# First weight unit of a decoder trunk split in halves on two engines, with the opening of TensorE reordered

## Chip, cores and metric

One core of a Trainium2 chip runs the whole program in one launch. The metric is device time in microseconds (us) of one execution, the median of several. Engines: TensorE (PE), VectorE (DVE), ScalarE (ACT), GpSimd (POOL) and SyncE (SP), which issues the transfers.

## What is computed

Two layers over 512 tokens of width 1024, all in float32. The opening, which the change touches, is the norm of the input and the first columns of the projection `w_in`:

```python
def rms_norm(x, g):
    xf = x.astype(jnp.float32)
    y = xf * lax.rsqrt(jnp.mean(xf * xf, axis=-1, keepdims=True) + NORM_EPS)
    return (y * g.astype(jnp.float32)).astype(x.dtype)

for l in range(DEPTH):                       # DEPTH = 2
    h = h + token_mixer(rms_norm(h, ln1_g[l]), w_in[l], ...)   # starts with u @ w_in
    h = h + hier_moe(rms_norm(h, ln2_g[l]), ...)
return rms_norm(h, final_g)
```

`token_mixer` holds four attention-like branches with gates, `hier_moe` a router and 32 experts.

## The kernel before

A float32 product is made of three fast matmuls (`mm3`, L568 to L570): each operand is split in a high part, rounded to the fast type, and a low part, the rest. High times high, high times low and low times high are summed in PSUM. So each weight unit and each tile of u needs a high part (a ScalarE copy) and a low part (a subtraction) ahead of its matmuls.

`w_in` is cut in units of 256 columns (1024 rows as 8 groups k of 128), which SyncE loads in a ring of four slots `raw`. `split_h(u)` on ScalarE writes `ringH`, `split_l(u)` on GpSimd writes `ringL` (in the same memory as `raw`). Unit 0 ("gv") is used by rows: its halves q = 0 and 1 work on token tiles 0, 1 and then 2, 3, 24 matmuls (8 k x 3) for each tile. Unit 1 ("ga", the low-rank columns) and all later units need all four tiles.

A token tile t (128 tokens) passes through these steps: square sums on ScalarE (`row_squares`), mean on VectorE (`mean_square`), the power -1/2 on GpSimd (`norm_scale`), scaling with the gain `g1` on VectorE (`first_rows`), 8 turns on PE (`norm_transposes`), high part on ScalarE (`norm_h`), low part on VectorE (`norm_low`).

Each engine's program is written out by hand as a sequence with semaphore waits, and an engine handles its instructions strictly in that order. In layer 0 ScalarE's order is: squares 0 and 1, `split_h(0)`, squares 2 and 3, `norm_h` 0 and 1, `split_h(1)`, `norm_h` 2 and 3, then the loop over halves, which begins with `split_h(2)`. GpSimd does scales 0 and 1, `split_l(0)`, scales 2 and 3, `split_l(1)`. PE turns tiles 0 and 1, then waits for the low parts of unit 0 and of tile 0, works on tile 0, turns tile 2 between tiles 0 and 1, and turns tile 3 ahead of tile 2. Layer 1 has orders of its own, since its opening is mixed with the end of layer 0: there half of unit 0 was already subtracted by VectorE (`next_unit_low`, signals `front_high` and `front_low`).

SyncE issues x tile 0, the small constants `cst`, unit 0, `g1`, x tiles 1 to 3, unit 1, ten small constants, units 2 and 3, and a copy of x to DRAM. It doesn't wait for any engine up to there but for x.

In the expert stage `keep_warm` (L934 before) issues matmuls of a constant whose result nobody reads.

## Time and profile before

| | us |
|---|---|
| median of 3 runs | 1482.52 (1477.93 to 1482.81) |
| profiled execution | 1481.1 |
| its span | 1479.3 |
| PE busy | 1395.6 (94%) |
| ACT busy | 473.6 (32%) |
| DVE busy | 430.4 (29%) |
| POOL busy | 489.8 (33%) |

All durations below come from the profiled execution; its clock starts at the span's start. A PE matmul's own duration holds its latency, so matmuls overlap: how fast they run is read from start to start.

### The profile page before, as it was taken

How to read it: one execution, taken by the hardware profiler on the slowest of the kernel's cores; microseconds unless marked ns; L12 is line 12 of the kernel's file. 1: busy time of each engine (PE TensorE's matmuls, PEld its weight loads, DVE VectorE, ACT ScalarE, POOL GpSimd, SP SyncE). 2: the span in 40 equal slices, each digit the busy share in tenths (PEclk: the TensorE clock that was granted, in tenths of full speed). 3: DMA queues.
4: the chain of work that ended last, by engine and by line, in shares of the span. 5: the costliest groups of instructions: out<-in, count | busy, mean ns of one | idle time of the engine just before them, and what ended most of it. 6: DMA issues, size and time to landing. Idle time of an engine off the chain costs nothing.

```text
span 1479.3 us, 18875 instructions
## 1 busy us (share of the span) xinstructions
PE 1395.6 (94%) x7502; PEld 969.5 (66%) x7502; DVE 430.4 (29%) x1042; ACT 473.6 (32%) x818; POOL 489.8 (33%) x241
## 2 busy tenths in 40 slices
PE   5999999999999898988999999999999989998986
PEld 5889877788888633333388888777888874333332
DVE  2232554410122312111333435443102141121114
ACT  4522466632332111111253326765223311111112
POOL 3633433456660111111144343335567301111111
PEclk9999999999999799999999999999999998999999
DMA  7522222224375899999963213222334669999996
GB/s 249 190 86 86 72 72 72 72 89 146 107 267 200 342 414 420 419 420 416 391 241 102 86 58 107 72 72 72 96 139 162 235 232 400 414 420 420 419 414 263
DMA packets 129154, 331.23 MB, mean 224 GB/s; under 512 B 16613, under 2 KB 90421, under 8 KB 105512
## 3 DMA queue, kind: packets, MB, share of 16 engines
q1 hardware_dynamic: 120424, 314.29, 55.7%
q0 software_dynamic: 8640, 15.69, 2.8%
q8 instruction: 62, 1.02, 0.3%
q14 instruction: 28, 0.23, 0.0%
HBM read 312.17 MB, written 33.55 MB: 234 GB/s over the span
## 4 chain that ended last, share of the span: by engine, by line
PE 77%; DMA 16%; DVE 2%; SPq 1%; ACT 1%; issue 1%; POOL 1%; POOLq 0%; DVEq 0%; ACTq 0%
PE ps L568 18%; PE ps L569 17%; PE ps L570 17%; PE ps L956 13%; DMA w<-in_w 12%; DMA yb<-y_dram 2%; PE ps L770 1%; PE ps L750 1%; PE ps L758 1%; PE ps L706 1%; PE ps L948 1%; SPq L467 1%; PE ps L867 1%; DMA x_dram<-hs 1%; DMA hs<-in_x 1%
## 5 line engine op out<-in xcount | busy, mean ns | idle before, releaser
L568 PE MATMUL ps<-uH,ringH 128*128 128x512 f32 x704 | 276.1, 392 | 0.0
L569 PE MATMUL ps<-uL,ringH 128*128 128x512 f32 x704 | 274.6, 390 | 0.0
L570 PE MATMUL ps<-uH,ringL 128*128 128x512 f32 x704 | 274.5, 390 | 0.0
L956 PE MATMUL ps<-w,xT 128*64 128x512 f32 x1024 | 229.0, 599 | 14.7 <-DMA w<-in_w 12.1
L956 PEld LDWEIGHTS ps<-w,xT 128*64 128x64 f32 x1024 | 77.1, 138 | 161.0 <-issue 152.8
L1370 POOL TENSOR_TENSOR ringL<-raw,ringH 128x2048 fp32r<-128x2048 f32 x29 | 133.3, 4606 | 81.8 <-ACT ringH L1098 81.8
L956 PE MATMUL ps<-w,hT 128*64 128x512 f32 x512 | 129.1, 650 | 30.2 <-DMA w<-in_w 18.9
L568 PEld LDWEIGHTS ps<-uH,ringH 128*128 128x128 f32 x704 | 132.6, 188 | 28.6 <-issue 0.7
L570 PEld LDWEIGHTS ps<-uH,ringL 128*128 128x128 f32 x704 | 132.4, 188 | 27.9
L569 PEld LDWEIGHTS ps<-uL,ringH 128*128 128x128 f32 x704 | 132.5, 188 | 27.1
L1416 POOL TENSOR_TENSOR ringL<-raw,ringH 128x2048 fp32r<-128x2048 f32 x32 | 147.1, 4597 | 5.4 <-ACT ringH L1239 5.4
L1447 POOL DMA_INDIRECT y_dram<-yy,toks x28 | 28.2, 1009 | 348.7 <-DVE yy L1904 327.6
L1313 ACT ACTIVATE silu<-ps,slot_w 128x256 f32<-128x256 f32 x32 | 15.1, 473 | 323.8 <-PE ps L956 323.8
L1419 POOL TENSOR_TENSOR merged<-merged,term 128x512 f32<-128x512 f32 x48 | 67.1, 1397 | 149.3 <-DVE term L1721 149.3
L956 PEld LDWEIGHTS ps<-w,hT 128*64 128x64 f32 x512 | 38.6, 148 | 98.3 <-issue 81.6
L1243 ACT ACTIVATE sig<-ps 128x512 f32<-128x512 f32 x64 | 38.3, 598 | 201.1 <-PE ps L570 201.0
L568 PE MATMUL ps<-ringH,uH 128*128 128x256 f32 x320 | 93.4, 292 | 3.5 <-POOL ringL L1370 2.5
L569 PE MATMUL ps<-ringL,uH 128*128 128x256 f32 x320 | 91.0, 284 | 0.0
L570 PE MATMUL ps<-ringH,uL 128*128 128x256 f32 x320 | 91.0, 284 | 0.0
L1721 DVE TENSOR_TENSOR term<-sig,ps 128x512 f32<-128x512 f32 x48 | 32.9, 686 | 198.3 <-PE ps L570 124.4
L1904 DVE SCALAR_TENSOR_TENSOR yy<-xg,first_choice,ps 128x512 f32<-128x512 f32 x56 | 39.3, 744 | 139.7 <-PE ps L956 139.7
L1860 DVE SCALAR_TENSOR_TENSOR hid<-silu,slot_w,ps 128x256 f32<-128x256 f32 x32 | 15.4, 480 | 211.1 <-ACT silu L1313 211.1
(266 smaller groups left out, 2076.5 us busy)
## 6 DMA issues: line engine op xcount, KB each, us to landing
w<-in_w SPq DMA_DIRECT2D x176, 1024.0 KB, 17.4
raw<-in_w_in SPq DMA_DIRECT2D x54, 1024.0 KB, 5.0
w<-in_w SPq DMA_DIRECT2D x32, 512.0 KB, 17.8
raw<-in_w_out SPq DMA_DIRECT2D x8, 1024.0 KB, 5.2
yb<-y_dram SPq DMA_DIRECT2D x8, 1024.0 KB, 15.7
braw<-in_w_branch SPq DMA_DIRECT2D x24, 256.0 KB, 4.4
h_dram<-hs SPq DMA_DIRECT2D x2, 2048.0 KB, 11.8
y_dram<-attT SPq DMA_DIRECT2D x8, 512.0 KB, 9.0
```

The lines of the kernel that those rows point to most:

```text
L568: mm(o, h, rh, start=first, stop=False)
L569: mm(o, h, rl_, start=False, stop=False)
L570: return mm(o, l, rh, start=False, stop=last)
L956: ins = mm(o[r], lhs[:, r], rhs[x], start=first, stop=last, skip_group_check=True)
L1243: fn(sig[:, j % 2, :], bank(b), ACT.Sigmoid).then_inc(bank_freed[b].h, 1)
L1370: gp_.tensor_tensor(ringL[:, s, :], raw[:, s, :], ringH[:, s, :].bitcast(f32), ALU.subtract).then_inc(unit_low.h, 1)
L1416: gp_.tensor_tensor(ringL[:, s, :], raw[:, s, :], ringH[:, s, :].bitcast(f32), ALU.subtract).then_inc(unit_low.h, 1)
L1419: gp_.tensor_tensor(merged[:, j, :], merged[:, j, :], term[:, j % 2, :], ALU.add).then_inc(term_added.h, 1)
L1447: gp_.indirect_dma_start(y_dram, bass.IndirectOffsetOnAxis(toks[:, 1, p:p + 1], axis=0), yy[:], None, bounds_check=2 * S - 1, oob_is_err=F ...
L1721: v.tensor_tensor(term[:, j % 2, :], sig[:, j % 2, :], bank(A[5]), ALU.mult).then_inc(term_ready.h, 1)
L1860: return v.scalar_tensor_tensor(hid[:], silu[:], slot_w[:, 0, col], bank(0)[:, FH:2 * FH], ALU.mult, ALU.mult)
L1904: last = v.scalar_tensor_tensor(yy[:, cc], xg[p % 3][:, cc], first_choice[:, p:p + 1], bank(A[c]), ALU.mult, ALU.add)
```

## The change

- SyncE issues `g1` ahead of unit 0.
- ScalarE, layer 0: unit 0 is split in two halves of 1024 columns (k 0 to 3, k 4 to 7). Order: squares 0, first half, `norm_h(0)`, squares 1, second half, squares 2 and 3, `norm_h(1)`, `split_h(1)`, `norm_h(2)`, `split_h(2)`, `norm_h(3)`. `split_h(2)` was behind `norm_h(3)`.
- VectorE subtracts both halves of unit 0 (`unit_low_half`); GpSimd's `split_l(0)` is gone.
- PE, layer 0: five keep-warm matmuls at the start and five behind the turns of tile 0. The turns of tiles 1 and 2 stand between k 3 and k 4 of tiles 0 and 1. PE waits for the first half of unit 0 ahead of tile 0 and for the second ahead of its k 4.
- `front_high` and `front_low` count one more, since layer 0 now uses them too. Layer 1's orders stay.

```diff
--- before.py
+++ after.py
@@ -269,7 +269,7 @@
     bank_filled = signal("bank_filled", NH + 40)
     NB0, NB1 = (NH + 1) // 2, NH // 2
     bank_freed = [signal("bank_freed0", NB0 + 20), signal("bank_freed1", NB1 + 20)]
-    front_high = signal("front_high", 1); front_low = signal("front_low", 1)
+    front_high = signal("front_high", 1, 1); front_low = signal("front_low", 1, 1)
     side_turned = signal("side_turned", 2); side_copied = signal("side_copied", 2)
     lowrank_ready = signal("lowrank_ready", 1)
     decay_arg = signal("decay_arg", 1)
@@ -364,8 +364,8 @@
     def _(sp):
         sp.dma_start(hs[:, 0, :], a["x"][0, 0:P, :]).then_inc(x_in[0].h, 16)
         sp.dma_start(cst[:], a["c_small"]).then_inc(cst_in.h, 16)
+        sp.dma_start(g1[:], a["ln1_g"][0:1, :].partition_broadcast(P)).then_inc(g1_in.h, 16)
         sp.dma_start(raw[:, 0, :].rearrange("p (k n) -> p k n", k=KD), w_in_cols(0, COL["gv"], 256)).then_inc(w_in_slot[0].h, 16)
-        sp.dma_start(g1[:], a["ln1_g"][0:1, :].partition_broadcast(P)).then_inc(g1_in.h, 16)
         for t in range(1, NT):
             sp.dma_start(hs[:, t, :], a["x"][0, t * P:(t + 1) * P, :]).then_inc(x_in[t].h, 16)
 
@@ -579,7 +579,13 @@
             pe.wait_ge(y_back[t].h, y_back[t].at(lay, 16))
             mm(bank(SUM_BANKS[x]), ident, yb[t][:, 1, cc], start=False, stop=True, skip_group_check=True).then_inc(sum_filled.h, 1)
 
+        def keep_warm(n, b):
+
+            for _ in range(n):
+                mm(bank(b, 256), ident, cst[:, 0:256], start=True, stop=True)
+
         pe.wait_ge(cst_in.h, 16)
+        keep_warm(5, 5)
         for lay in range(L):
 
             def norm_transposes(n, dst_free):
@@ -596,7 +602,7 @@
 
             norm_transposes(0, rows_low)
             if lay == 0:
-                norm_transposes(1, rows_low)
+                keep_warm(5, 5)
             else:
                 token_rows(5, 0, True, False)
                 token_rows(5, 1, False, False)
@@ -604,12 +610,11 @@
                 other_rows(lay - 1, 5)
 
             def second_tile():
-                if lay:
-                    norm_transposes(1, rows_low)
-                    for x in (6, 7):
-                        token_rows(x, 0, True, False)
-                        token_rows(x, 1, False, False)
-                        other_rows(lay - 1, x)
+                norm_transposes(1, rows_low)
+                for x in (6, 7):
+                    token_rows(x, 0, True, False)
+                    token_rows(x, 1, False, False)
+                    other_rows(lay - 1, x)
                 norm_transposes(2, rows_low)
 
             def half(q):
@@ -618,8 +623,9 @@
                 n = UNITS[u][1]
                 wH = ringH[:, s, 0:KD * n].rearrange("p (k n) -> p k n", k=KD)
                 wL = ringL[:, s, 0:KD * n].rearrange("p (k n) -> p k n", k=KD)
-                pe.wait_ge(unit_low.h, unit_low.at(lay, u + 1))
-                if u == 0 and lay:
+                if u or lay:
+                    pe.wait_ge(unit_low.h, unit_low.at(lay, u + 1))
+                if u == 0:
                     pe.wait_ge(front_low.h, front_low.at(lay - 1, 1))
                 if q >= 2:
                     pe.wait_ge(bank_freed[b].h, bank_freed[b].at(lay, q // 2))
@@ -635,7 +641,7 @@
                 else:
                     for i in range(2):
                         if q < 2:
-                            if q == 0 and i == 1:
+                            if q == 0 and i == 1 and lay:
                                 second_tile()
                             if q == 1 and i == 0 and lay == 0:
                                 norm_transposes(3, rows_low)
@@ -643,6 +649,10 @@
                         for k in range(KD):
                             if q == 1 and i == 0 and k == 4 and lay:
                                 norm_transposes(3, rows_low)
+                            if q == 0 and k == 4 and lay == 0:
+                                norm_transposes(i + 1, rows_low)
+                                if q == i == 0:
+                                    pe.wait_ge(unit_low.h, unit_low.at(0, 1))
                             last = mm3(ps[:, b * 512 + i * n:b * 512 + (i + 1) * n], uH[:, k, tmc(2 * off + i)],
                                        uL[:, k, tmc(2 * off + i)], wH[:, k, :], wL[:, k, :], k == 0, k == KD - 1)
                 last.then_inc(bank_filled.h, 1)
@@ -931,15 +941,10 @@
             def list_weights(rhs):
                 return list_product(lambda x: rhs[:, x].rearrange("p a e -> p (a e)"), 384, 2 * NP)
 
-            def keep_warm(n):
-
-                for _ in range(n):
-                    mm(bank(A[0], 256), ident, cst[:, 0:256], start=True, stop=True)
-
-            keep_warm(2)
+            keep_warm(2, A[0])
             pe.wait_ge(list_weights_ready.h, list_weights_ready.at(lay, 1))
             list_weights(w_rhs).then_inc(list_weights_filled.h, 1)
-            keep_warm(6)
+            keep_warm(6, A[0])
 
 
             def transpose_rows(src):
@@ -1120,11 +1125,13 @@
 
             row_squares(0)
             if lay == 0:
+                act.wait_ge(w_in_slot[0].h, w_in_slot[0].at(0, 16))
+                fn(ringH[:, 0, 0:1024], raw[:, 0, 0:1024], ACT.Copy).then_inc(front_high.h, 1)
+                norm_h(0)
                 row_squares(1)
-                split_h(0)
+                fn(ringH[:, 0, 1024:2048], raw[:, 0, 1024:2048], ACT.Copy).then_inc(unit_high.h, 1)
                 row_squares(2)
                 row_squares(3)
-                norm_h(0)
                 norm_h(1)
             else:
                 norm_h(0)
@@ -1138,6 +1145,7 @@
             split_h(1)
             if lay == 0:
                 norm_h(2)
+                split_h(2)
                 norm_h(3)
 
             def k2_rows(br):
@@ -1177,7 +1185,7 @@
 
             for q in range(NH):
                 kind, u, off, name = HALVES[q]
-                if q == 0 or HALVES[q - 1][1] != u:
+                if (q == 0 and lay) or (q and HALVES[q - 1][1] != u):
                     split_h(u + 2)
                 if name == "ga":
                     act.wait_ge(s_cst.h, 16 * N_CST)
@@ -1375,8 +1383,6 @@
 
             for t in range(NT):
                 norm_scale(t)
-                if lay == 0 and t == 1:
-                    split_l(0)
             split_l(1)
             if lay == 0:
                 hold(pool, s_cst.h, 16 * N_CST)
@@ -1512,10 +1518,27 @@
             v.tensor_tensor(uL[:, :, tmc(t)], ps[:, b * 512:b * 512 + 1024].rearrange("p (k n) -> p k n", k=KD),
                             uH[:, :, tmc(t)].bitcast(f32), ALU.subtract).then_inc(rows_low.h, 1)
 
+        def unit_low_half(c):
+
+            cc = slice(c * 1024, (c + 1) * 1024)
+            if c == 0:
+                dve.wait_ge(front_high.h, front_high.at(-1, 1))
+            else:
+                dve.wait_ge(unit_high.h, unit_high.at(0, 1))
+            v.tensor_tensor(ringL[:, 0, cc], raw[:, 0, cc], ringH[:, 0, cc].bitcast(f32), ALU.subtract).then_inc((front_low, unit_low)[c].h, 1)
+
         mean_square(0, 0)
         first_rows(0, 0)
+        unit_low_half(0)
+        norm_low(0, 0)
         mean_square(0, 1)
         first_rows(0, 1)
+        mean_square(0, 2)
+        unit_low_half(1)
+        first_rows(0, 2)
+        norm_low(0, 1)
+        mean_square(0, 3)
+        first_rows(0, 3)
 
         for lay in range(L):
             links = [0]
@@ -1528,12 +1551,6 @@
 
 
             if lay == 0:
-                norm_low(0, 0)
-                mean_square(0, 2)
-                first_rows(0, 2)
-                norm_low(0, 1)
-                mean_square(0, 3)
-                first_rows(0, 3)
                 norm_low(0, 2)
                 norm_low(0, 3)
                 dve.wait_ge(s_cst.h, 16 * N_CST)
```

ScalarE in the opening of layer 0, before (`junk` squares, `ringH` weight splits, `uH` high parts of tiles, `vv` the results of unit 0):

```order
L1081 ACTIVATE junk,ss<-hs 128x1024 [waits squares_summed,x_in1]
L1098 ACTIVATE ringH<-raw 128x2048 [waits w_in_slot0]
L1081 ACTIVATE junk,ss<-hs 128x1024 [waits squares_summed,x_in2]
L1081 ACTIVATE junk,ss<-hs 128x1024 [waits squares_summed,x_in3]
L1111 ACTIVATE uH<-ps 128x8x128 [waits rows_turned] x2
L1096 ACTIVATE ringH<-raw 128x8x16 [waits w_in_slot1,squares_summed]
L1111 ACTIVATE uH<-ps 128x8x128 [waits rows_turned] x2
L1098 ACTIVATE ringH<-raw 128x2048 [waits w_in_slot2]
L1106 ACTIVATE vv<-ps 128x512 [waits bank_filled] x2
```

The same place now:

```order
L1129 ACTIVATE ringH<-raw 128x1024 [waits w_in_slot0]
L1116 ACTIVATE uH<-ps 128x8x128 [waits rows_turned]
L1086 ACTIVATE junk,ss<-hs 128x1024 [waits squares_summed,x_in1]
L1132 ACTIVATE ringH<-raw 128x1024
L1086 ACTIVATE junk,ss<-hs 128x1024 [waits squares_summed,x_in2]
L1086 ACTIVATE junk,ss<-hs 128x1024 [waits squares_summed,x_in3]
L1116 ACTIVATE uH<-ps 128x8x128 [waits rows_turned]
L1101 ACTIVATE ringH<-raw 128x8x16 [waits w_in_slot1,squares_summed]
L1116 ACTIVATE uH<-ps 128x8x128 [waits rows_turned]
L1103 ACTIVATE ringH<-raw 128x2048 [waits w_in_slot2]
L1116 ACTIVATE uH<-ps 128x8x128 [waits rows_turned]
L1111 ACTIVATE vv<-ps 128x512 [waits bank_filled] x2
```

Unit 0's split and the high part of tile 0 moved ahead of the squares of tile 1, and the split that waits for unit 2 (`w_in_slot2`) moved ahead of the last tile's high part.

VectorE at the start now (before, the same without the two `ringL` rows, and with `ms`, `ut` of tile 1 ahead of the first `uL`):

```order
L1508 TENSOR_SCALAR ms<-ss 128x1 [waits squares_summed]
L1504 SCALAR_TENSOR_TENSOR ut<-hs,rstd,g_94 128x1024 [waits scale_ready,g1_in]
L1528 TENSOR_TENSOR ringL<-raw,ringH 128x1024 [waits front_high]
L1518 TENSOR_TENSOR uL<-ps,uH 128x8x128 [waits rows_high]
L1508 TENSOR_SCALAR ms<-ss 128x1 [waits squares_summed]
L1504 SCALAR_TENSOR_TENSOR ut<-hs,rstd,g_94 128x1024 [waits scale_ready]
L1508 TENSOR_SCALAR ms<-ss 128x1 [waits squares_summed]
L1528 TENSOR_TENSOR ringL<-raw,ringH 128x1024 [waits unit_high]
L1504 SCALAR_TENSOR_TENSOR ut<-hs,rstd,g_94 128x1024 [waits scale_ready]
L1518 TENSOR_TENSOR uL<-ps,uH 128x8x128 [waits rows_high]
```

The norm of tile 1 (`ut`) now stands behind the low part of tile 0 (`uL`), and that of tile 2 behind the second half of unit 0.

## Rows read from the trace of the kernel before

**Rows 1.** The page: span, PE's busy time, shares of the chain.
```profile
span 1479.3 us, 18875 instructions
PE 1395.6 (94%) x7502; PEld 969.5 (66%) x7502; DVE 430.4 (29%) x1042; ACT 473.6 (32%) x818; POOL 489.8 (33%) x241
...
PE 77%; DMA 16%; DVE 2%; SPq 1%; ACT 1%; issue 1%; POOL 1%; POOLq 0%; DVEq 0%; ACTq 0%
```
**Rows 2.** Chain of waits, 0 to 60 us: start, duration, what.
```profile
2.74 9.27 DMA hs<-in_x
12.03 1.15 ACT junk L1081 x2
13.18 1.81 ACT ringH L1098
15.16 4.65 POOL ringL L1370
19.90 0.55 PE ps L568
```
**Rows 3.** Timeline of PE: start, duration, line, out<-in, [idle before <-releaser].
```profile
19.90 0.55 PE L568 MATMUL ps<-ringH,uH 128*128 128x256 f32 x1 [2.45 <-POOL ringL L1370]
...
22.17 0.41 PE L569 MATMUL ps<-ringL,uH 128*128 128x256 f32 x1
22.39 0.41 PE L570 MATMUL ps<-ringH,uL 128*128 128x256 f32 x1
22.60 0.34 PE L568 MATMUL ps<-ringH,uH 128*128 128x256 f32 x1
22.78 0.28 PE L569 MATMUL ps<-ringL,uH 128*128 128x256 f32 x1
...
31.59 0.28 PE L568 MATMUL ps<-ringH,uH 128*128 128x256 f32 x1
...
34.46 0.39 PE L629 MATMUL ps<-uH,ringH 128*32 128x512 f32 x1
```
**Rows 4.** Issues of cst, unit 0, g1, x tile 1, unit 2: KB, us to landing.
```profile
cst<-in_c_small SPq DMA_DIRECT2D x1, 272.0 KB, 3.9
raw<-in_w_in SPq DMA_DIRECT2D x1, 1024.0 KB, 7.5
g<-in_ln_g SPq DMA_DIRECT2D x1, 512.0 KB, 8.6
hs<-in_x SPq DMA_DIRECT2D x1, 512.0 KB, 9.3
raw<-in_w_in SPq DMA_DIRECT2D x1, 1024.0 KB, 9.7
```
**Rows 5.** Timeline of DVE and POOL, 0 to 60 us.
```profile
10.77 1.28 DVE L1498 SCALAR_TENSOR_TENSOR ut<-hs,rstd,g 128x1024 f32<-128x1024 f32 x1 [5.02 <-DMA g<-in_ln_g]
18.21 1.22 DVE L1512 TENSOR_TENSOR uL<-ps,uH 128x1024 fp32r<-128x1024 f32 x1 [2.79 <-ACT uH L1111]
29.96 1.23 DVE L1512 TENSOR_TENSOR uL<-ps,uH 128x1024 fp32r<-128x1024 f32 x1 [2.52 <-ACT uH L1111]
...
13.55 0.55 POOL L1374 TENSOR_TENSOR rstd<-ms,cst 128x1 f32<-128x1 f32 x1 [6.98 <-DVE ms L1502]
15.16 4.64 POOL L1370 TENSOR_TENSOR ringL<-raw,ringH 128x2048 fp32r<-128x2048 f32 x1 [1.06 <-ACT ringH L1098]
```
**Rows 6.** Timeline of PE in the expert stage, keep-warm matmuls at half clock.
```profile
1227.44 3.19 PE L937 MATMUL ps<-cst 128*128 128x256 f32 x7
```
**Rows 7.** Timeline of ACT, the last tile's high part and the split of unit 2.
```profile
28.91 1.02 ACT L1111 ACTIVATE uH<-ps 128x1024 fp32r<-128x1024 f32 x1 [2.72 <-PE ps L593]
29.83 1.91 ACT L1098 ACTIVATE ringH<-raw 128x2048 fp32r<-128x2048 f32 x1
```
**Rows 8.** PE behind pauses in the expert stage; then windows (PE, ..., PEclk, DMA, GB/s).
```profile
1310.22 4.99 PE L956 MATMUL ps<-w,hT 128*64 128x512 f32 x16 [2.50 <-DMA w<-in_w]
640.04 5.35 PE L956 MATMUL ps<-w,hT 128*64 128x512 f32 x16 [3.33 <-DMA w<-in_w]
655.75 3.65 PE L956 MATMUL ps<-w,hT 128*64 128x512 f32 x16 [1.91 <-DMA w<-in_w]
...
582.50:589.30 6.80, 4.86 (x12) 1.65 (x14) 0.00 (x0) 0.00 (x0) 0.00 (x0) 0.50 1.01 416
655.70:657.00 1.30, 1.25 (x6) 0.57 (x8) 0.00 (x0) 0.00 (x0) 0.00 (x0) 1.00 1.07 438
1309.00:1313.00 4.00, 2.78 (x8) 1.05 (x10) 0.00 (x0) 0.17 (x1) 0.00 (x0) 0.57 1.03 422
```

## Prediction

> **What bounds the kernel now.** The page comes first: TensorE (PE) is busy for 94% of the span and holds 77% of the chain that ended last, DMA 16% [rows 1]. So a change is worth what it lets PE finish earlier. The change touches only the opening of layer 0, so the chain of waits is read there next: from 2.74 to 19.9 us it runs over a transfer of x, a row of squares, the ScalarE split of unit 0, the 4.65 us GpSimd subtraction, and only then PE [rows 2]. From 19.90 on PE has hardly a pause: the 24 matmuls of token tile 3 start at 31.59, and the next unit starts at 34.46 [rows 3]. I take 34.46 as the end of unit 0. Whatever that moment gains is gained to the end, because from there on order and waits are as before, and the refills are issued on PE's own milestones. The opening also shows matmuls of 0.41 us each until 22.39 and of 0.28 us from 22.78, start to start 0.21 and 0.12 us: PE was at its half clock of 1.2 GHz and reached 2.4 GHz at 22.6 [rows 3]. The clock column of the page reads full in these first microseconds, so there the durations are the evidence.
>
> **The change part by part.** I rebuild the opening with the durations of the rows.
>
> *Gain factors ahead of unit 0.* cst was issued at 1.18 and landed 3.9 us later, at 5.1; unit 0 at 1.64 and 7.5, so 9.1; g1 at 2.12 and 8.6, so 10.7; the second tile of x at 2.74 and 9.3, so 12.0 [rows 4]. They land in the order of issue, and g1 took 1.6 us behind unit 0. Swapped, g1 lands at 5.1 + 1.6 = 6.7 and unit 0 at 9.1 + 1.6 = 10.7; x is where it was. The first norm then runs at 6.7 instead of 10.77 and takes 1.28 us [rows 5], to 8.0.
>
> *Keep-warm matmuls.* 5 + 5 of 128x256 are added. One is two matmul records, and records of this kind stand 0.43 us apart at half clock (3.19 us for 7, the last one's latency in it) [rows 6]: 0.86 us each, 4.3 us for five. The first five hold PE from 5.1 to 9.4 and the turns of tile 0 behind them, ready at 8.2, wait 1.2 us. That costs nothing, since ScalarE is not free for the copy of those turns before 11.7 (below). They raise the clock earlier; full speed for 13 matmuls is worth 13 x 0.09 = 1.2 us [rows 3].
>
> *Unit 0 by halves.* ScalarE splits 1024 columns at 10.7 in some 1.0 us (a 1024-wide copy took 1.02) [rows 7], to 11.7. VectorE subtracts that half. No row shows this operation; its neighbours are a 1024-wide subtraction from PSUM, 1.22, and half of GpSimd's 4.64 for 2048 [rows 5]. I take 1.22 because it is the same engine and operation, and keep 2.3 as the far end. So 13.0. The copy of tile 0 on ScalarE ends at 12.7, its low part on VectorE at 14.2, and PE starts unit 0 at 14.3 in place of 19.90: 5.6 us sooner.
>
> *What is late next.* Square sums of tile 1 end at 13.9; VectorE takes them behind the low part at 14.2, GpSimd's scale takes 0.55 [rows 5], the norm of tile 1 runs 15.1 to 16.4, and its turns 16.5 to 17.5. The second half's subtraction ends at 17.7, after the wait for squares 2 that stands ahead of it. PE: tile 0, k 0 to 3, 14.3 to 15.8; pause; turns to 17.5; k 4 to 7, 17.8 to 19.3. Low part of tile 1 at 20.1, PE on it until 24.0 with turns of tile 2 inside, turns of tile 3 until 24.9, tile 2 from 24.9 to 27.9. Taken alone this would be the gain: tile 3 could start at 27.9, 3.7 us before 31.59.
>
> *The wait that takes its place.* `split_h(2)` now stands between `norm_h(2)` and `norm_h(3)` on ScalarE, and waits for the transfer of unit 2. That was issued at 16.37 and took 9.7 us: it lands at 26.1 [rows 4]. SyncE's issues after the swap are untouched and wait for nothing that the change moves, so 26.1 stays. Before, this wait was met long ago when ScalarE came to it (29.83) [rows 7]. Now ScalarE is there at 23.6 and sits idle for 2.5 us with `norm_h(3)` queued behind. From 26.1: split 1.91, copy of tile 3 1.02, low part 1.23, about 0.1 between, gives 30.3 for PE's tile 3 [rows 5, 7]. Its matmuls take 34.46 - 31.59 = 2.87, so unit 0 ends at 33.2. **Gain 1.2 us**, not 3.7. A slower half subtraction, a late g1 or keep-warms at half clock all end inside the 2.4 us that PE now waits. GpSimd's half of unit 2 ends at 28.1 + 4.6 = 32.7, before its use at some 37, so it costs nothing.
>
> *The clock in that wait.* PE idles from 27.9 to 30.3. In the expert stage a 2.50 us pause for weights was followed by 16 matmuls in 4.99 us where 3.65 is normal, the granted clock of that stretch being 0.57, and a 3.33 us pause by 5.35; after a 1.91 us pause the 16 took 3.65 at clock 1.00 [rows 8]. So the price is between 0 and 1.7 us. I take 1.3, from the 2.50 us pause, which is nearest to my 2.4.
> The Trainium skill (TensorE: Matmul & The Clock Gate, Part 1) says that the number of slow matmuls differs from run to run of the same kernel. By that page neither 0 nor 1.3 is the whole answer, and the sum would be 1479.9 us in some executions and 1481.2 in others; one execution of before can't show it.
>
> **Sum.** The profiled execution took 1481.1 us (span 1479.3 plus 1.8 around it). 1481.1 - 1.2 + 1.3 = 1481.2 us. The median of the runs shown is 1.4 above that execution, and the runs spread over 4.9 us. About 0.5% (7.4 us) is what a measurement of this kernel tells from no change, so the forecast is **no change**.
>
> **The rivals.**
> *The clean gain.* Unit 2 lands before 23.6, or ScalarE's order does not matter, and tile 3 starts at 27.9: 1481.1 - 3.7 = 1477.4 us. For it: the rest of the chain allows it. Against it: the landing row, and an issue order that nothing moves. A chance of 0.15.
> *Slower.* The pause lets the clock fall for a stretch like the one of 6.8 us at clock 0.50 [rows 8], in which 6.8 us do the work of 3.4. That falls on tile 3 and the low-rank unit behind it: 1481.1 - 1.2 + 3.4 = 1483.3 us. It decides once more than 2.4 us of matmuls run at half clock. For it: two kinds of fall stand in the rows. Against it: PE is dense behind the pause, as it was from 19.90, where full clock came after 2.7 us. A chance of 0.12.
> *Nothing arrives.* Unit 2 lands 1.2 us later than in this trace, at 27.3, or the shift is lost in a later transfer: 1481.1 us. The transfers of the expert stage are issued on PE's milestones, which speaks against a loss there. A chance of 0.08.
>
> **How the numbers follow.** The forecast (gated by unit 2, clock price 0 to 1.7, so 1479.9 to 1481.6) has 0.65. Likeliest 1481.2. The range reaches down to the clean gain and up to the slower rival, with the bit that a median of few runs can lie off: 1476.5 to 1483.8. Every case lies within 0.5%: same 0.95; 0.03 for faster and 0.02 for slower are for what I don't see.
>
> **What would show it.** Right: the first 128x256 matmul near 14.3; ScalarE idle until about 26.1 ahead of the 128x2048 split of unit 2, released by DMA; PE idle for 2 to 3 us ahead of tile 3; the low-rank unit at about 33.2 or 34.5 in place of 34.46; GpSimd without its first 4.6 us subtraction. Wrong: unit 2's transfer landing before 24; no PE pause ahead of tile 3; the low-rank unit below 32; or a difference that arises after 35 us.

## The result, and the profile after

The changed kernel took 1485.66 us (median of 20 runs, 1481.03 to 1489.63), the kernel before beside it 1482.12 (20 runs, 1477.93 to 1484.86): ratio 1.0027, 95% interval 1.0018 to 1.0036. Slower by 3.5 us, where the prediction had 1481.2 and a range that ended at 1483.8. That is less than the 0.5% that the prediction named as the bound of "no change", but outside its range. In both kernels the executions spread over 7 to 9 us, so one traced execution shows where time goes and not what the median gains.

The page of the changed kernel: a longer span with the same shares of the chain, and 20 matmuls more (before: [rows 1]).

```profile
span 1484.6 us, 18915 instructions
PE 1402.5 (94%) x7522; PEld 975.1 (66%) x7522; DVE 435.9 (29%) x1044; ACT 474.4 (32%) x819; POOL 486.1 (33%) x240
...
PE 77%; DMA 16%; DVE 2%; ACT 1%; SPq 1%; issue 1%; POOL 0%; POOLq 0%; DVEq 0%; ACTq 0%
```

**The opening did what was forecast, about half as well.** Timeline of TensorE from the start (columns as in [rows 3]):

```profile
5.45 4.63 PE L585 MATMUL ps<-cst 128*128 128x256 f32 x10 [5.45 <-DMA cst<-in_c_small]
9.88 1.09 PE L599 MATMUL ps<-cst,ut 128*128 128x128 f32 x8
10.81 2.32 PE L585 MATMUL ps<-cst 128*128 128x256 f32 x10
14.90 0.36 PE L568 MATMUL ps<-ringH,uH 128*128 128x256 f32 x1 [1.76 <-DVE uL L1518]
...
30.86 0.36 PE L568 MATMUL ps<-ringH,uH 128*128 128x256 f32 x1 [1.68 <-DVE uL L1518]
...
33.80 0.39 PE L635 MATMUL ps<-uH,ringH 128*32 128x512 f32 x1
```

The first five keep-warm matmuls (ten records) run at half clock and fill the time to 9.88; the second five take half as long for the same work, so full clock was reached before unit 0. Unit 0 starts at 14.90 in place of 19.90. Ahead of tile 3 PE waits 1.68 us. The low-rank unit, my mark for the end of unit 0, starts at 33.80 against 34.46 [rows 3]: 0.66 us sooner.

The same stretch on VectorE, then on ScalarE, answers to [rows 5] and [rows 7]:

```profile
8.01 1.28 DVE L1504 SCALAR_TENSOR_TENSOR ut<-hs,rstd,g 128x1024 f32<-128x1024 f32 x1 [1.92 <-DMA g<-in_ln_g]
...
12.39 1.23 DVE L1528 TENSOR_TENSOR ringL<-raw,ringH 128x1024 fp32r<-128x1024 f32 x1 [3.10 <-ACT ringH L1129]
13.54 1.22 DVE L1518 TENSOR_TENSOR uL<-ps,uH 128x1024 fp32r<-128x1024 f32 x1
```
```profile
11.31 1.06 ACT L1129 ACTIVATE ringH<-raw 128x1024 fp32r<-128x1024 f32 x1 [5.40 <-DMA raw<-in_w_in]
...
23.65 1.03 ACT L1116 ACTIVATE uH<-ps 128x1024 fp32r<-128x1024 f32 x1 [4.38 <-PE ps L599]
26.64 1.92 ACT L1103 ACTIVATE ringH<-raw 128x2048 fp32r<-128x2048 f32 x1 [1.96 <-DMA raw<-in_w_in]
28.46 1.00 ACT L1116 ACTIVATE uH<-ps 128x1024 fp32r<-128x1024 f32 x1
```

ScalarE sits idle for 1.96 us until unit 2 has landed, with the last tile's high part queued behind: the wait that the prediction named.

**The loss arises 700 us later.** The prediction had named this as a sign of being wrong, "a difference that arises after 35 us". Timeline of TensorE at the end of layer 0, first before, then in the changed kernel; L574, L575 and L580 sum the experts' results for the tokens (`token_rows`, `other_rows`):

```profile
731.72 0.50 PE L574 MATMUL ps<-yH,tok_of 128*128 128x512 f32 x1
732.07 0.39 PE L575 MATMUL ps<-yL,tok_of 128*128 128x512 f32 x1
732.69 1.12 PE L580 MATMUL ps<-yb,cst 128*128 128x512 f32 x2 [0.23 <-DMA yb<-y_dram]
```
```profile
729.68 0.50 PE L574 MATMUL ps<-yH,tok_of 128*128 128x512 f32 x1
730.01 0.40 PE L575 MATMUL ps<-yL,tok_of 128*128 128x512 f32 x1
733.90 2.07 PE L580 MATMUL ps<-yb,cst 128*128 128x512 f32 x2 [3.50 <-issue]
734.99 1.41 PE L574 MATMUL ps<-yH,tok_of 128*128 128x512 f32 x1
736.20 0.63 PE L575 MATMUL ps<-yL,tok_of 128*128 128x512 f32 x1
```

The changed kernel comes here 2.04 us ahead (729.68 against 731.72) and leaves L580 1.21 us behind (733.90 against 732.69): a pause of 3.50 us for which the profile names no releaser, only "issue". The chain of waits at this place gives the same reading; the data that L580 uses had landed at 730.60:

```profile
715.39 15.21 DMA yb<-y_dram
730.60 3.31 issue
733.90 2.07 PE ps L580 x2
```

Behind the pause the granted clock is half. Windows of the changed kernel, the pause and then the 3.1 us after it (PE, PEld, DVE, ACT, POOL busy, PEclk, DMA share, GB/s):

```profile
730.40:733.90 3.50, 0.01 (x1) 0.00 (x0) 0.69 (x1) 0.93 (x1) 2.34 (x1) 0.96 1.02 419
733.90:737.00 3.10, 3.10 (x5) 1.83 (x6) 0.69 (x1) 0.00 (x0) 0.00 (x0) 0.50 1.04 368
```

3.1 us at half clock do the work of 1.55. Matching the two traces matmul by matmul, the changed kernel goes from 2.2 us ahead (650 us) to 2.7 behind (738 us). Only 0.66 of the 2.2 is the opening; the rest is a fall of the clock near 146 us that was shorter in this execution (below). The remainder of the 5.3 us by which its span is longer is a fall of the clock near 877, which costs 3.1 us; the stretches behind it give 0.6 back.

### The profile page after: what moved, and what is told of

Its sections match the earlier page's. It is cut to its first block, busy times and chain, and to the rows that moved or that the text cites. A ratio compares the mean times of both kernels' runs of the same rounds, so it can differ in the third digit from the quotient of the medians.

```text
span 1484.6 us, 18915 instructions
## 1 busy us (share of the span) xinstructions
PE 1402.5 (94%) x7522; PEld 975.1 (66%) x7522; DVE 435.9 (29%) x1044; ACT 474.4 (32%) x819; POOL 486.1 (33%) x240
## 4 chain that ended last, share of the span: by engine, by line
PE 77%; DMA 16%; DVE 2%; ACT 1%; SPq 1%; issue 1%; POOL 0%; POOLq 0%; DVEq 0%; ACTq 0%
PE ps L568 17%; PE ps L569 17%; PE ps L570 17%; PE ps L961 13%; DMA w<-in_w 12%; DMA yb<-y_dram 2%; PE ps L780 1%; PE ps L760 1%; PE ps L768 1%; PE ps L716 1%; PE ps L953 1%; PE ps L877 1%; DMA x_dram<-hs 1%; DMA raw<-in_w_in 1%; DMA xg<-x_dram,toks 1%
## 5 line engine op out<-in xcount | busy, mean ns | idle before, releaser
L961 PEld LDWEIGHTS ps<-w,xT 128*64 128x64 f32 x1024 | 78.1, 139 | 159.6 <-issue 152.4
L961 PE MATMUL ps<-w,hT 128*64 128x512 f32 x512 | 126.1, 637 | 33.6 <-DMA w<-in_w 21.8
L1378 POOL TENSOR_TENSOR ringL<-raw,ringH 128x2048 fp32r<-128x2048 f32 x28 | 128.7, 4603 | 83.0 <-ACT ringH L1103 83.0
L1422 POOL TENSOR_TENSOR ringL<-raw,ringH 128x2048 fp32r<-128x2048 f32 x32 | 147.0, 4594 | 5.1 <-ACT ringH L1247 5.1
```

The source lines that it names most:

```text
L961: ins = mm(o[r], lhs[:, r], rhs[x], start=first, stop=last, skip_group_check=True)
L1378: gp_.tensor_tensor(ringL[:, s, :], raw[:, s, :], ringH[:, s, :].bitcast(f32), ALU.subtract).then_inc(unit_low.h, 1)
L1422: gp_.tensor_tensor(ringL[:, s, :], raw[:, s, :], ringH[:, s, :].bitcast(f32), ALU.subtract).then_inc(unit_low.h, 1)
```

## Why TensorE had nothing to execute

Two things stand next to the pause. The first is a branch of TensorE's own program, L355, which every engine takes once in each layer, here past 245 of TensorE's instructions for further windows of the expert list that do not occur. In both layers it took about 0.35 us, as in the kernel before, and in layer 0 it ended 5.7 us before the pause did (durations in ns: shortest, median, longest; then first and last start in us):

```profile
L355 PEldq COMPARE_BRANCH  x2: 333/346/358, 727.8 to 1462.0; - x2
```

The second is one of the two queues that bring the engines their instructions (q8 on the page: 62 transfers, MB, share of time):

```profile
q8 instruction: 62, 1.02, 0.3%
```

One of its transfers, 16,384 bytes, 0.95 us long, started at 731.56 inside the pause, 3.73 us after the branch began, and ended 1.39 us before TensorE went on. No other transfer of instructions lay between the branch and 733.9 but a short one (8,192 bytes) on the second instruction queue at 729.66. That q8 serves TensorE is inferred: 62 blocks of 256 are 15,872 instructions, about the length of its program, and the transfers stand some 256 of its instructions apart.

The places below are counts of TensorE's instructions in the built programs. Ten keep-warm matmuls are 40 instructions (each is two matmul records, [rows 6], and each record has its weight load). With them one wait instruction is gone, the one ahead of the first turns, so all of TensorE's code behind the opening stands 39 places later; the traces agree, 15,378 records of TensorE against 15,339. The trace shows that exactly eight instructions ran behind the branch: four of control, and weight load and matmul of L574 and of L575. The ninth, the weight load of L580, waited.

With blocks of 256 instructions (16,384 bytes at 64 each) this puts the edge of a block eight places behind the branch's target, and 47 behind it before the change. The edge ahead of that one lies 3 places before the branch in the changed kernel, and 36 places behind the branch before it. So TensorE entered the block that holds both branch and target just before it branched, jumped over nearly all of it, and was at its end before the next had come. In the kernel before it enters that block by the branch itself, but then has 47 instructions to do: it reached the 48th at 737.74, and the next block had landed at 734.91. That is a theory with a number in it: what moves TensorE's code by as much as the change does must bring the pause, wherever the instructions come from.

The Trainium skill (Runtime: NRT & Kernel Launch, Instruction fetch mechanics) says that each engine's sequencer fetches its program in 16 KiB blocks of 256 instructions, and that a taken branch whose target lies outside the window of two blocks must wait for the fetch. The size agrees with the 16,384 bytes in this trace. The rule about the target is not what this trace shows: the target was there, and eight instructions ran; the block behind it was not.

Theories for the experiments: **position** (the keep-warm matmuls' number of instructions moves the edge), **content** (the keep-warm matmuls or the new opening bring the pause through the clock or through an earlier arrival; the expectations call this "phase"), and, apart from these, how much of the opening's loss belongs to the early `split_h(2)`.

## The experiments

### The change without its keep-warm matmuls

```diff
         pe.wait_ge(cst_in.h, 16)
-        keep_warm(5, 5)
...
-            if lay == 0:
-                keep_warm(5, 5)
-            else:
+            if lay:
                 token_rows(5, 0, True, False)
```

> The change without its ten keep-warm matmuls in the opening; all else of the change stays. PE's program is then 39 instructions shorter, exactly as long as in the kernel before, and its branch at the end of layer 0 stands where it stood. Theory 'code position' (PE waits for a block of its own instructions behind that branch, because the 39 added instructions moved the edge of a block close behind it): the 3.5 us pause ahead of the sum matmuls at 734 us is gone, the opening still ends at 33.8 to 34.5 us, and the time is the kernel before less 0 to 0.7: a ratio to before of 0.9995 to 1.0000, some 1481.8 us. Rival 'phase' (an opening that ends at another moment puts the later stages at another moment of the clock and the transfers): the opening is as in the change, so the time stays near 1485.7, ratio 1.002 to 1.003. Rival 'keep-warm pays' (without them the clock in the opening is half and tile 0 slower): the opening ends later than 34.5 us.

Measured: 1480.28 us against 1482.76, ratio 0.9984 (0.9971 to 0.9998), a little below the 0.9995 to 1.0000 expected. TensorE's program is exactly as long as before (15,339 records). The pause at the end of layer 0 is gone:

```profile
729.23 1.13 PE L580 MATMUL ps<-yb,cst 128*128 128x512 f32 x2 [0.17 <-DMA yb<-y_dram]
```

The opening is slower in its matmuls and no later in its end, as the half clock is hidden by waits (ahead of tile 3 TensorE now waits 0.80 us in place of 1.68):

```profile
9.86 1.94 PE L598 MATMUL ps<-cst,ut 128*128 128x128 f32 x8 [9.86 <-DVE ut L1501]
15.01 0.55 PE L568 MATMUL ps<-ringH,uH 128*128 128x256 f32 x1 [3.22 <-DVE uL L1515]
...
33.88 0.39 PE L632 MATMUL ps<-uH,ringH 128*32 128x512 f32 x1
```

33.88 against 33.80 with them. So the keep-warm matmuls bring at most 0.1 us here (in the pair with the split put back, below, the order is reversed: 32.52 with them, 32.16 without), and they take some 6 us of the whole (0.9984 against 1.0027). The gain of 0.16%, 2.5 us, is more than the 0.58 us of the opening, and no run shows where the rest comes from. The trace has no half clock near 146 us, which is worth 3.2 us in it, but neither has that of the kernel before with 40 waits.

### The kernel before with 40 waits that are met at once

```diff
         pe.wait_ge(cst_in.h, 16)
+        for _ in range(40):
+            hold(pe, s_init.h, 1)
         for lay in range(L):
```

> The kernel before with 40 waits on a semaphore that is met long ago, at the start of PE's program; no other edit. They are handled by PE's sequencer while PE waits for the first norm. PE's program is as long as the changed kernel's and its branches stand where they stand there. 'Code position': a pause of 3 to 4 us ahead of the sum matmuls at the end of layer 0 that no data explains, and the time is before plus 3.5 to 5: 1485.6 to 1487 us, ratio 1.0024 to 1.0034. 'Phase': opening and everything behind it are as before, ratio 1.000.

Measured: 1486.60 us against 1482.76, ratio 1.0027 (1.0014 to 1.0041), the change's own ratio with none of its edits. The 40 waits lengthen TensorE's program by 39 records, as the change does, since the separate wait instruction ahead of the first turns is gone here too. The opening ends at 34.37, as before. The pause is there:

```profile
729.83 0.50 PE L574 MATMUL ps<-yH,tok_of 128*128 128x512 f32 x1
730.17 0.40 PE L575 MATMUL ps<-yL,tok_of 128*128 128x512 f32 x1
733.00 1.91 PE L580 MATMUL ps<-yb,cst 128*128 128x512 f32 x2 [2.43 <-issue]
```
```profile
733.00:736.60 3.60, 3.60 (x7) 1.87 (x7) 0.69 (x1) 0.00 (x0) 1.02 (x1) 0.53 1.01 387
```

It stands at the same instruction, the ninth behind the branch, with the block of instructions arriving from 730.54 to 731.50 and half clock behind it. This decides between position and content. One caution: the profiled execution was the fastest of this kernel's twelve (1482.27), so its trace shows the pause and a loss of 3.8 us there, but not what makes the median 4 us longer than that execution.

### The early split of unit 2 put back

```diff
                 norm_h(2)
-                split_h(2)
                 norm_h(3)
...
-                if (q == 0 and lay) or (q and HALVES[q - 1][1] != u):
+                if q == 0 or HALVES[q - 1][1] != u:
                     split_h(u + 2)
```

> The change with the split of unit 2 back behind the high part of tile 3 on ScalarE; keep-warm stays. Prediction's term 'the wait that takes its place': tile 3 starts at 28 us in place of 30.9, the low-rank unit at 31 in place of 33.8, and the time falls by 2.5 to 3 against the change: ratio to before 1.0003 to 1.0013. The 3.5 us pause at the end of layer 0 stays ('code position', PE's program is as long as in the change) and under 'phase' may go. If unit 2's split were not what tile 3 waits for, the opening would not move.

Measured: 1483.48 us, ratio 1.0006 (0.9995 to 1.0018). The low-rank unit starts at 32.52, 1.3 us sooner than in the change where 2.8 was expected, with no wait ahead of tile 3, and the pause stays, since ScalarE's order does not move TensorE's code:

```profile
732.94 2.07 PE L580 MATMUL ps<-yb,cst 128*128 128x512 f32 x2 [3.73 <-issue]
```

The ratio falls by 0.21%, 3.1 us, which is more than the opening gives.

### Both: no keep-warm matmuls, and the split put back

> Both: no keep-warm, and unit 2's split behind the high part of tile 3. 'Code position': no pause at the end of layer 0, the opening ends at 31 to 31.8 us, and the time is before less 2.5 to 3.4: 1478.7 to 1479.6 us, ratio 0.9977 to 0.9983, the fastest of all. 'Phase': no figure follows; anything from 0.998 to 1.003.

Measured: 1479.68 us, ratio 0.9983 (0.9971 to 0.9996). The low-rank unit starts at 32.16, 2.3 us before [rows 3], with no pause in layer 0. It is faster than both kernels. The 1.7 us that it has over the version with the early split (33.88) do not show in the medians (0.9983 against 0.9984), while with the keep-warm matmuls the same move brought 3.1 us. The intervals, over 0.2% wide, allow both to be the 1.3 to 1.7 us of the openings; what the early split costs in the median is not shown more closely.

### The gain factors behind unit 0 again, on that version

```diff
-        sp.dma_start(g1[:], a["ln1_g"][0:1, :].partition_broadcast(P)).then_inc(g1_in.h, 16)
         sp.dma_start(raw[:, 0, :].rearrange("p (k n) -> p k n", k=KD), w_in_cols(0, COL["gv"], 256)).then_inc(w_in_slot[0].h, 16)
+        sp.dma_start(g1[:], a["ln1_g"][0:1, :].partition_broadcast(P)).then_inc(g1_in.h, 16)
```

> No keep-warm, late split, and the gain factors again behind unit 0 in SyncE's order: only the swap undone. By the prediction's landings: unit 0 lands at 9.1 to 9.6 in place of 11.2, g1 at 10.7 to 11.2, the first norm ends at 12 to 12.5, the turns of tile 0 at 14, PE starts unit 0 at 16.3 to 16.8 in place of 14.8, and the low-rank unit starts 0.5 to 1.6 us later than at 32.2. If the order of the two transfers did not matter, the start of unit 0 stays at 14.8.

One execution only, and a little more than expected: the turns of tile 0 start at 12.67 in place of 9.86, unit 0 at 17.08 in place of 14.75, the low-rank unit at 34.38 in place of 32.16. Without the swap nearly the whole lead of 2.3 us is gone: the split into halves needs the first norm to be early. The openings of single traces differ, though: that of this version with keep-warm matmuls ended at 32.52, and with 20 more waits, below, at 31.17.

### Twenty more waits, on both kernels

20 instructions more, ahead of the wait for `cst`, in the change, in the change with the split put back, and in the kernel before.

```diff
+        for _ in range(20):
+            hold(pe, s_init.h, 1)
         pe.wait_ge(cst_in.h, 16)
```

> The change with 20 more waits (met long ago) at the start of PE's program, and nothing else: more instructions, no less work. 'Code position': instructions are fetched in blocks of 16 KB (the size of the transfers on the instruction queue), 256 of 64 bytes. The pause stood some 8 instructions behind the branch target (number 7869 in my count of PE's program), so an edge lies near 7877. With 20 more the target is at 7889, behind the edge, and the next edge is over 240 instructions away: no pause, time falls by 3.5 to 5 against the change, to 1480.7 to 1482.2 us, ratio to before 0.9990 to 1.0000. Rival 'length' (any longer PE program, or the work of more instructions, costs): 1486 us or more, ratio 1.0027 to 1.004. Rival 'phase': no reason to move, 1.0027.

> The change with unit 2's split behind the high part of tile 3, and 20 more waits as in the last. 'Code position': no pause; opening ends at 32.2 to 32.7 us as without the pads; the time is that of the kernel without keep-warm and with the late split, 1479 to 1480 us, ratio 0.9977 to 0.9990. Rivals 'length' and 'phase': 1483.5 or more, ratio 1.0006 or more.

> The kernel before with 20 waits in place of 40: the target of the branch is at 7850, the edge at 7877 is 27 instructions behind it, which is in the third to sixth group of the sum matmuls, reached 2 to 4 us later than in the kernel with 40. 'Code position': a pause of 0 to 1.5 us in place of 2.4, and it stands later in the sum matmuls than the first group of other rows; time before plus 0 to 1.5, ratio 1.000 to 1.001. 'Length': half of what 40 cost, ratio 1.0013.

The kernel before followed the theory to the instruction: the 28th behind the branch waited. 1482.78 us, ratio 0.9999 (0.9989 to 1.0009), and a short pause at the place forecast, where the edge of the block stands 27 places behind the target:

```profile
736.92 0.40 PE L574 MATMUL ps<-yH,tok_of 128*128 128x512 f32 x1
737.78 0.50 PE L575 MATMUL ps<-yL,tok_of 128*128 128x512 f32 x1 [0.46 <-issue]
```

The change did not. I had expected it to be cured, and it took 1488.43 us, ratio 1.0037 (1.0025 to 1.0049), where the rival "length" had put it; with the split put back 1484.60, ratio 1.0009 (0.9996 to 1.0022). The branch itself now took 3.9 us (shortest, median and longest of its two executions):

```profile
L355 PEldq COMPARE_BRANCH  x2: 223/2078/3933, 727.4 to 1458.7; - x2
```
```profile
731.91 0.47 PE L574 MATMUL ps<-yH,tok_of 128*128 128x512 f32 x1 [2.67 <-issue]
```

Here the branch stands 23 places inside one block and its target 12 places inside the next. So the stall had not gone, it had moved from the instruction behind the edge to the branch: the block that was late is now the target's own. It landed at 729.94, and the branch ended 1.40 us later. Matmuls that were already queued ran on during the branch, so TensorE stood idle for 2.67 us of the 3.93, with full clock behind it, and the trace loses only 2.2 us at this place (the change: 4.7).

That does not explain the median. This trace is of the fastest of nine executions (1483.17), and no trace shows what makes the median 5.3 us longer; 0.7 us of the difference to the change is a later unit 2 in the opening (low-rank unit at 34.49). In layer 1 the count puts the target three places ahead of an edge in these two kernels; TensorE pauses 1.42 and 1.25 us there, but behind six instructions, not three. Where the count is off is not known.

### 104 places further in all

The change with 65 waits, the same with the split put back, and the kernel before with 104: three kernels with TensorE's code at the same place.

> The change with 65 more waits (met long ago) at the start of PE's program: three times the pads of the kernel that was slowest so far. 'Code position', as the last runs mended it: PE takes its code in blocks of 256 instructions; a block is sent for when PE enters the one before it, and is there some 5 us later. Edges lie at 7621, 7877 and 15557, 15813 of my count. With 65 the branches stand at 7689 and 15610, 68 and 53 instructions behind an edge, so the block that holds their targets (7934, 15855) has come when the branch is taken, and the next edge is 200 instructions away. No pause, the branch itself takes 0.2 to 0.4 us, and the time is that of the change without keep-warm: 1480 to 1482 us, ratio to before 0.998 to 0.9998. Rival 'length': slower than with 20 pads, ratio 1.004 or more.

> As the last, with unit 2's split behind the high part of tile 3. 'Code position': no pause, the opening ends 1.3 to 3 us sooner than in the last (31.2 to 32.5 us), time 1478.5 to 1480, ratio 0.997 to 0.9985, the fastest with keep-warm in it. 'Length': ratio 1.001 or more.

> The kernel before with 104 waits at the start of PE's program (handled in some 5 us while PE waits for the first norm at 12 us): the same branch positions as in the two kernels above, no other edit. 'Code position': ratio 0.9995 to 1.0005, no pause that data don't explain at either branch. 'Length' (40 pads cost 0.27%, in proportion 104 cost 0.7%): 1.007.

Results: 1483.18 us, ratio 1.0008 (0.9994 to 1.0022); 1486.22, ratio 1.0014 (1.0001 to 1.0027); 1486.44, ratio 1.0010 (0.9995 to 1.0026). Two things went another way than I wrote. A wait that is met (and sets a signal of its own, as these do) costs about 0.15 us, not 0.05: with 65 of them the keep-warm matmuls began at 10.84 in place of 5.45, so that these ratios hold a later opening too (low-rank unit at 35.08, 36.15 and 36.41). All three ratios lie above what "position" expected, and far below the 1.004 and 1.007 of the rival "length" for the first and the third, which these two runs speak against. And the branch was quick in only one of the three in layer 0:

```profile
L355 PEldq COMPARE_BRANCH  x2: 355/1952/3550, 728.2 to 1455.4; - x2
```
```profile
L355 PEldq COMPARE_BRANCH  x2: 3850/4071/4292, 730.3 to 1463.9; - x2
```

The first is the change with 65, the second the same with the split put back. The first's quick execution is the one in layer 0; in layer 1, where a quick branch was expected too, all three took 3.55 to 3.85 us, of which the trace of the change with 65 loses 1.0 us. In the first a block of instructions had been sent for at 722.02, 6.2 us before the branch; in the other two none was sent for from 694 until 732.27 and from 693 until 731.09, after the branch had begun (730.33 and 729.56). If a block is sent for when TensorE enters the one ahead of it, the first is what 68 places of advance should give, and the other two are not. What decides it is not settled by these runs. It need not be the kernel: the trace with the quick branch is of the fastest of that kernel's twelve executions (1480.34, where the slowest took 1490.15), and each kernel has one trace.

### The change with only the first five keep-warm matmuls

The same move of the code as twenty waits on the kernel before, but in the changed kernel and with real keep-warm matmuls.

```diff
             if lay == 0:
-                keep_warm(5, 5)
+                pass
             else:
```

> The change with the second five keep-warm matmuls left out, the first five kept: 20 instructions fewer on TensorE, so its code stands 19 instructions later than in the kernel before, about where the kernel before with 20 added waits had it. Theory of the position of the code (TensorE waits for a block of its own instructions when such a block ends 8 instructions behind the branch target, as with 39 or 40 more, and for at most half a microsecond when it ends 27 or 28 behind): the pause at the end of layer 0 is 0.0 to 0.6 us instead of 3.5, the branch itself takes 0.36 us, the opening ends as in the change (low-rank unit 33.7 to 34.3 us), ratio to before 0.998 to 0.9995. Rival, the keep-warm matmuls or the new opening bring the pause in by another way than their number of instructions: pause 3 us or more at the first sum of the tokens, ratio 1.002 to 1.003. Rival from the runs with 20 more on the changed kernel, where the branch took 3.9 us: a stall can come at any position, then the branch takes over 3 us and the ratio is 1.002 or more.

Measured: 1480.03 us against 1482.55, ratio 0.9982 (0.9973 to 0.9991). The branch took 0.36 us, the low-rank unit starts at 33.93, and the pause is that of the kernel before with 20 waits, at the same matmul and of the same length; with 19 places in place of 20 the 29th instruction waited and not the 28th:

```profile
730.95 1.12 PE L580 MATMUL ps<-yb,cst 128*128 128x512 f32 x2 [0.27 <-DMA yb<-y_dram]
...
734.55 0.39 PE L575 MATMUL ps<-yL,tok_of 128*128 128x512 f32 x1 [0.46 <-issue]
```

Leaving out five matmuls in the first 15 us took 0.45% off the time. The kernel is faster than both, and not to be told from the one without any.

### All positions together

Places are counted in TensorE's own instructions, the branch of the kernel before being number 7585 and its target 7830. The edges of blocks, 256 apart, are inferred from where TensorE paused. The wait is the one at the end of layer 0 in the profiled execution; "lost" is what the trace loses against that of the kernel before from 725 to 745 us, matmul by matmul, half clock included.

| kernel | moved by | branch from edge 7621 | target from edge 7877 | TensorE waits | lost | ratio |
|---|---|---|---|---|---|---|
| before | 0 | 36 ahead | 47 ahead | none | | 1 |
| change, no keep-warm | 0 | 36 ahead | 47 ahead | none | 0.0 | 0.9984 |
| same, split put back | 0 | 36 ahead | 47 ahead | none | 0.0 | 0.9983 |
| change, five keep-warm | 19 | 17 ahead | 28 ahead | 0.46 | 0.6 | 0.9982 |
| before, 20 waits | 20 | 16 ahead | 27 ahead | 0.46 | 0.7 | 0.9999 |
| change | 39 | 3 behind | 8 ahead | 3.50 | 4.7 | 1.0027 |
| change, split put back | 39 | 3 behind | 8 ahead | 3.73 | 6.4 | 1.0006 |
| before, 40 waits | 39 | 3 behind | 8 ahead | 2.43 | 3.8 | 1.0027 |
| change, 20 waits | 59 | 23 behind | 12 behind | branch 3.93 | 2.2 | 1.0037 |
| same, split put back | 59 | 23 behind | 12 behind | branch 3.75 | 2.0 | 1.0009 |
| change with 65, same with split put back, before with 104 | 104 | 68 behind | 57 behind | branch 0.36, 4.29, 3.89 | 0.0, 4.2, 3.8 | 1.0008, 1.0014, 1.0010 |

Up to 39 the reading is plain: the fewer instructions stand between the target and the edge at 7877, the longer the wait, since the block behind that edge lands some 5 us after the branch (in the kernel before its transfer started at 733.95, 4.06 us after the branch, and took 0.96; there TensorE had 47 instructions to do). The three kernels at 39 wait at the same instruction and differ by when the transfer started, 2.39 us after the branch where the wait was 2.43, and 3.73 and 3.97 where it was 3.50 and 3.73. At 59 and 104 the block behind that edge holds the target, and the branch waits for it in four of five profiled executions.

One number ties the waits to the transfers. In all nine traces with a wait at the end of layer 0, from 0.46 to 4.29 us long, TensorE went on 1.38 to 1.50 us after the block had landed. Where there was no wait, as in the kernel before, TensorE came to the edge later than that.

## Why the prediction was wrong

**The step that failed is "Keep-warm matmuls", with its sentence "That costs nothing".** I priced ten matmuls by their time on TensorE and their place in the opening, where they are indeed free (33.80 against 33.88 without them). What they cost lies in their number as instructions: 40 of them, less one wait, shift everything behind, and at the end of layer 0 TensorE then waits for its own program, 3.5 us, and runs at half clock for 3.1 us after it, another 1.55. Shown by the kernel before with 40 idle waits (1.0027) and by the change with fewer or no keep-warm matmuls (0.9982, 0.9984). That term was missing from the sum, and from the bounds and the rivals as well; its size, from these ratios, is 4 to 7 us. The sentence "from there on order and waits are as before" was true of the order written in the code and false of the waits. That the measured 1485.66 lies near the "slower" rival's 1483.3 is no credit to it: that rival put its loss on tile 3.

The other steps:

- *Gain factors ahead of unit 0*: right in kind. g1 landed at 7.9 and unit 0 at 11.3, not 6.7 and 10.7: 1.2 and 0.6 late. Undoing the swap cost 2.2 us of opening, in one trace.
- *Unit 0 by halves*: the half subtraction took 1.23 against the 1.22 taken. PE started at 14.90 against 14.3, and the 0.6 is unit 0's landing.
- *What is late next*: PE reached tile 3's place at 29.2, not 27.9; most of it is that PE began tile 1 at 21.07, not 20.1, itself partly the late start of unit 0.
- *The wait that takes its place*: right, and its mechanism shown by taking it away. ScalarE waited 1.96 us for unit 2, which was there at 26.6, not 26.1: its transfer took 9.7 us as before but was issued at 16.93 in place of 16.37, so SyncE's times were not quite untouched. Unit 0 ended at 33.80, so the gain was 0.66 where I had 1.2. Of the clean gain of 3.7 the version with the split put back and no keep-warm matmuls reached 2.3, and its best relative, the one with keep-warm matmuls and 20 waits, 3.3.
- *The clock in that wait*: I took 1.3 us; it was 0. Behind a pause of 1.68 us tile 3's matmuls stood 0.12 us apart, full clock, as behind the 1.91 us pause in [rows 8]. The row nearest to the pause that came would have been the right one; I had chosen by the pause that I forecast, 2.4. But in the change with 20 waits the pause was 2.25 us and tile 3 still ran at full clock (2.93 us for its 24 matmuls), so the length of the pause alone does not tell.
- The sentence on the Trainium skill (TensorE: Matmul & The Clock Gate, Part 1), that the number of slow matmuls differs from run to run, was not needed at tile 3, and no kernel here has two traces to test it. Falls elsewhere do differ between nearly equal kernels: in attention the half clock lasted from 145.6 to 152.4 in the kernel before and from 146.4 to 149.9 in the changed one, and in the kernel before with 40 waits the granted clock was 1.00 from 140 to 152. So nothing ties the 1.5 us that the changed trace gains there to the change.

What stays open. Near 877 the changed kernel falls to half clock for 6.8 us (3.1 us lost) and the profiled execution of before does not:

```profile
877.00:883.80 6.80, 6.80 (x30) 5.88 (x30) 1.86 (x5) 3.33 (x5) 1.97 (x1) 0.50 0.15 51
```

It stands in six of the 14 traces. It is there with five keep-warm matmuls as well, at a ratio of 0.9982, and not with 40 waits on the kernel before or with the split put back, so it does not go with the pause. What brings it on was not tried. Also open is why the loss between no keep-warm matmuls and ten (0.43%) is larger than that by 40 waits alone (0.27%); their intervals allow both to be equal. And the waits explain the times only up to 39 places: at 59 the trace loses less than in the change, and the median is the slowest of all.

## What to carry to other kernels

In a long program with a taken branch, an edit's instructions can have a price apart from their time: they move all later code of that engine against the edges of the blocks in which it is fetched. Look behind every branch for a pause that the profile puts down to "issue", compare its time with the instruction queue's transfers, and before judging an edit by its ratio, run the old kernel with as many idle instructions as the edit adds (count them in the trace: 40 waits in the source were 39 more here). When two halves of an edit are judged together, a small loss can hide a small gain: here the change is worth 0.18% once five idle matmuls are left out of it, and costs 0.27% with them.

## What the runs showed of the hardware

- TensorE waited 2.4 to 3.7 us for a block of its instructions that begins eight places behind the target of a taken branch (three kernels), 0.46 us at 27 and 28 places, and not at 47. A block is 16,384 bytes. Its transfer took 0.95 to 0.97 us and started 2.4 to 4.1 us after the branch, and TensorE went on 1.38 to 1.50 us after it had ended.
- With the branch 23 or 68 places inside a block and its target in the next one, the branch itself took 3.75 to 4.29 us at the end of layer 0 in four of five profiled executions, and 0.36 in the fifth; in layer 1, 53 places inside, 3.55 to 3.85 us in three of three. TensorE's matmuls stood still for 2.5 to 3.0 us of the four. With the branch 16 to 36 places ahead of the edge and its target in the next block it took 0.36.
- Behind the waits at eight places the clock was at half for 3.1, 3.4 and 6.2 us; behind the four slow branches for 3.4 us in two traces (104 places) and not at all in two (59 places).
- A wait that is already met, and sets a signal, cost TensorE about 0.15 us at the start of the program: with 65 of them its first matmul came at 10.84 us, and with 104 at 16.97.
